# Dilated attention: values with v as the weights, two heads on the column halves of TensorE's array, output turned back by two transposes per double unit

## What is computed

```python
s = einsum('bnqche,bnkche->bnchqk', qs, kw) * scale + bias
s = where(mask, s, MASK_VALUE)
m = max(s, axis=-1)
e = exp(s - m)
l = sum(e, axis=-1)
o = einsum('bnchqk,bnkche->bnqche', e, vw)
o = o * (1 / l)
lse = m + log(l)
```

## Time and profile before

| | |
|---|---|
| median of 3 runs | 3131.64 us (3131.01 to 3131.96) |
| profiled execution | 3134.61 us, span 3132.8 us |
| mean granted TensorE clock | 0.977 |
| TensorE matmuls / weight loads | 2984.1 us (95%) / 2489.8 us (79%) |
| VectorE / ScalarE / POOL | 1656.2 (53%) / 1195.8 (38%) / 729.7 us (23%) |
| dilated attention on TensorE | 1392.9 to about 1751 us |
| its value matmuls (L1354) | 1280 records, 163.9 us |

### The profile page before, as it was taken

How to read it: one execution, slowest core, us unless ns; L and a number is a source line. 1 busy time by engine, 2 the same in 40 slices (tenths; PEclk the granted TensorE clock), 3 DMA queues, 4 the chain that set the end, 5 groups by cost and what they waited for, 6 DMA issues and landing times. The chain is left out here.

```text
span 3132.8 us, 47888 instructions
## 1 busy us (share of the span) xinstructions
PE 2984.1 (95%) x18330; PEld 2489.8 (79%) x18330; DVE 1656.2 (53%) x2757; ACT 1195.8 (38%) x2667; POOL 729.7 (23%) x576
## 2 busy tenths in 40 slices
PE   6999999999799999989999799899799999799998
PEld 6988888988588888878888678688688888667776
DVE  3366665000888888866666677433341100166665
ACT  3222221011577777755555321322211111255553
POOL 1234433110502010027452344200001110121111
PEclk9999999999899999999999899999899999899999
DMA  4212212223212010022332556332245542544341
GB/s 155 84 58 71 72 60 78 72 64 74 82 28 50 22 48 22 22 77 86 100 101 68 200 211 240 128 123 82 82 124 118 126 96 52 159 150 140 127 152 64
DMA packets 254270, 302.94 MB, mean 97 GB/s; under 512 B 19376, under 2 KB 201696, under 8 KB 250848
## 3 DMA queue, kind: packets, MB, share of 16 engines
q1 hardware_dynamic: 254048, 299.92, 31.7%
HBM read 190.38 MB, written 109.47 MB: 96 GB/s over the span
## 5 line engine op out<-in xcount | busy, mean ns | idle before, releaser
L890 DVE CUSTOM_DVE_ANT_0 d_e<-d_score,d_dist,d_slope 128x1024 f32<-128x1024 f32 x256 | 318.5, 1281 | 62.9 <-PE d_score L953 62.9
L561 PE MATMUL p_acc<-p_h_hi,p_w_hi 128*128 128x512 f32 x768 | 300.0, 391 | 1.0 <-issue 1.0
L561 PE MATMUL p_acc<-p_h_hi,p_w_lo 128*128 128x512 f32 x768 | 299.5, 390 | 0.0
L561 PE MATMUL p_acc<-p_h_lo,p_w_hi 128*128 128x512 f32 x768 | 299.1, 389 | 0.0
L812 ACT ACTIVATE d_e<-d_e,d_neg_top 128x2048 f32<-128x2048 f32 x128 | 257.0, 2008 | 86.5 <-DVE d_neg_top L899 86.2
L504 DVE RECIPROCAL p_root<-p_root 128x512 f32<-128x512 f32 x64 | 214.6, 3353 | 123.0 <-ACT p_root L417 123.0
L976 PE MATMUL d_out<-d_v,d_w_t 128*128 128x128 f32 x2048 | 251.5, 277 | 0.0
L976 PEld LDWEIGHTS d_out<-d_v,d_w_t 128*128 128x128 f32 x2048 | 240.9, 194 | 0.0
L561 PE MATMUL s_acc<-s_h_hi,s_w_hi 128*128 128x512 f32 x576 | 224.7, 390 | 0.0
L561 PE MATMUL s_acc<-s_h_hi,s_w_lo 128*128 128x512 f32 x576 | 224.4, 390 | 0.0
L561 PE MATMUL s_acc<-s_h_lo,s_w_hi 128*128 128x512 f32 x576 | 224.4, 390 | 0.0
(11 more groups left out here) (277 smaller groups left out, 6907.4 us busy)
## 6 DMA issues: line engine op xcount, KB each, us to landing
k_carry<-in_w_in SPq DMA_DIRECT2D x16, 1024.0 KB, 6.0
cols<-k_carry SPq DMA_DIRECT2D x64, 256.0 KB, 2.4
w_q<-q SPq DMA_DIRECT2D x15, 1024.0 KB, 7.8
k_carry<-x SPq DMA_DIRECT2D x27, 512.0 KB, 3.6
o_parts<-l_stage SPq DMA_DIRECT2D x192, 66.0 KB, 1.7
m_o<-o_parts SPq DMA_DIRECT2D x48, 264.0 KB, 6.0
k_carry<-cols SPq DMA_DIRECT2D x48, 256.0 KB, 4.6
k_carry<-in_a_w_in SPq DMA_DIRECT2D x10, 1024.0 KB, 5.6
```

Of the source, the lines that this page charges most:

```text
L561: mm = pe.matmul(acc[:, room], w_part[:, j, kt, ct * P:(ct + 1) * P], h_part[:, kt, tc * BANK:(tc + 1) * BANK], start=(kt == 0 and m == 0) ...
L890: dve.tensor_tensor_reduce(e[:, m % 3, s, half * HALF:(half + 1) * HALF], score[:, 2 * half:2 * half + 2].rearrange("p a b -> p (a b)"), d ...
```

## The change

The operands of the value matmuls change places: `v[level][:, chunk + k, own]` (128 keys x 64 channels) is the weight, `e_t` (128 keys x 128 queries) streams. Head h writes the partitions of its half, `own`, so that the two heads stand on the two column halves of the array. `out` now holds channels x queries for both units (`WIN` = 256 columns). VectorE copies it to the new tile `by_channel`; two transposes turn it back into the second half of the same bank; a second copy goes to `stage`. These steps run one round later, and the loops of VectorE and TensorE are a round longer. Two semaphores are new.

```diff
+        by_channel = ph.sb("by_channel", [P, WIN])
...
             def move_out(n):
                 dve.wait_ge(valued, 2 * n + 2)
+                if n >= 1:
+                    dve.wait_ge(turned_back, n)
+                dve.tensor_copy(by_channel[:, :], out[:, n % 2, 0:WIN]).then_inc(out_moved, 1)
+
+            def stage_out(n):
+                dve.wait_ge(turned_back, n + 1)
                 dve.tensor_copy(stage[:, 2 * n % SLOTS:2 * n % SLOTS + 2, 0:2 * HD],
-                                out[:, n % 2, 0:4 * HD].rearrange("p (u n) -> p u n", u=2)).then_inc(staged, 1)
-
-            for n in range(-1, TOTAL + 1):
+                                out[:, n % 2, WIN:2 * WIN].rearrange("p (u n) -> p u n", u=2)).then_inc(staged, 1)
+
+            for n in range(-1, TOTAL + 2):
+                if n >= 2:
+                    move_out(n - 2)
                 if n + 1 < TOTAL:
                     top(n + 1)
+                if n >= 2:
+                    stage_out(n - 2)
                 if 0 <= n < TOTAL:
                     for u in (2 * n, 2 * n + 1):
                         if not moved_by_act(u):
                             move(u)
-                if n >= 1:
-                    move_out(n - 1)
...
-                for h in range(2):
-                    for k in range(w):
-                        mm = pe.matmul(out[:, n % 2, (2 * j + h) * HD:(2 * j + h + 1) * HD], e_t[:, u % 4, w * h + k],
-                                       v[level][:, chunk + k, h * HD:(h + 1) * HD], start=(k == 0), stop=(k == w - 1))
+                for k in range(w):
+                    for h in range(2):
+                        own = slice(h * HD, (h + 1) * HD)
+                        mm = pe.matmul(out[own, n % 2, j * P:(j + 1) * P], v[level][:, chunk + k, own],
+                                       e_t[:, u % 4, w * h + k], start=(k == 0), stop=(k == w - 1))
                 mm.then_inc(valued, 1)

-            for n in range(-1, TOTAL + 1):
+            def turn_back(n):
+                pe.wait_ge(out_moved, n + 1)
+                for j in range(2):
+                    mm = pe.transpose(out[:, n % 2, WIN + j * P:WIN + (j + 1) * P], by_channel[:, j * P:(j + 1) * P],
+                                      ident[:, :])
+                mm.then_inc(turned_back, 1)
+
+            for n in range(-1, TOTAL + 2):
                 if n + 1 < TOTAL:
                     scores(n + 1)
+                if n >= 2:
+                    turn_back(n - 2)
                 for j in range(2):
                     if 0 <= n < TOTAL:
                         transposes(2 * n + j)
-                    if n >= 1:
+                    if 1 <= n <= TOTAL:
                         values(2 * n - 2 + j)
```

More of the change, by code:

```diff
@@ L1097, in dilated_attention @@
         valued = ph.sem("valued")
+        out_moved = ph.sem("out_moved")
+        turned_back = ph.sem("turned_back")
         staged = ph.sem("staged")
```

## The result

The changed kernel takes 3147.6 us (median of 7 runs, 3139.2 to 3156.3) against 3132.0 (3129.0 to 3139.1). The ratio is 1.0045, 95% interval 1.0029 to 1.0061: 9 to 19 us slower, 14 in the middle. The forecast was 19 us slower, at the edge of that interval, and 3150.5 us in all, 2.9 above the median and with it in the range of 3143 to 3170. The profiled executions differ by more than the ratio says, 3148.9 against 3132.8 us of span; 15.5 of these 16.1 us lie in dilated attention (first to last record: 1385.0 to 1751.5 before, 1386.0 to 1767.9 after), 1.0 came before it and the rest of the kernel gave back 0.3. What is outside is scatter: over the kernels of this study, in which the stages ahead of dilated attention are all the same, it starts anywhere between 1378.5 and 1389.2 us. So the stage's own length and its steps say more than a total.

The account below looks back on a forecast made before the run. TensorE's own queue was taken to bound the stage. Two-tile steps +2.6, single-tile steps +15.0 and the end +1.0 gave +18.6, say +19 us, on 3131.6: 3150.5 us, range 3143 to 3170.

Parts of the forecast that it names:

- What bounds the stage: Dilated attention: TensorE's own queue alone sets its time, matmuls filling 348.2 of 348.8 us.
- The change of division: TensorE's array: after a change the next group starts 0.07 us before the last matmul's recorded end, instead of 0.28.
- The pace of a pair: Value matmuls on the column halves: 0.115 us a pair, so groups take 0.60 us (4 pairs) or 0.37 (2).
- Two-tile steps: The 64 steps with two key tiles: 2.60 instead of 2.56 us from scores to bias, +0.04 each, +2.6 us.
- Single-tile steps: The 32 steps with one key tile: 1.70 instead of 1.23 us from scores to bias, +0.47 each, +15.0 us.
- The end: After the last values group: two transposes and a second copy are added before the store, +1.0 us.
- What was costed at nothing: VectorE's 96 more copies, 0.42 us each, 40 us in the stage, stay covered with 0.7 us slack; DMAs unchanged.
- Rival 1: Changes of division into or out of column halves cost nothing, values overlap as now: -42 us, 3090 us; chance 0.06.
- Rival 2: Value pairs do not keep 0.115 us at 128 columns: +29 us (3179) or +67 us (3217); chance 0.07.
- rival 3: VectorE's chain through by_channel becomes late in the fullest steps: some 3157 to 3163 us; chance 0.04.
- theory A: Follow-up runs: how often TensorE changes its array's division decides; a way into the column halves and out costs some 0.29 us.
- rival C: Run with e_t split into query halves: a pair never goes below about 0.11 us, ratio about 1.01; no chance given.

Follow-up runs that it names:

- the two-step blocks: Two kernels, mixed old/new value forms and e_t split into query halves, with two steps' values in one block instead of one step's: 1.0040 and 0.9944 to before.
- grouped_new: Changed kernel with both units' transposes together, then both units' values, entering the column halves once a step: 3121.7 us, 0.9961 to the kernel before.
- grouped_old: Kernel before the change, values in their old form, with the same regrouping (all transposes of a step, then all values): 1.0013 to the kernel before.
- heads_outer: Changed kernel with value matmuls in the other order, both key tiles of head 0, then both of head 1: 1.0049 to the kernel before.

## Why the prediction was right, point by point

- **What bounds the stage: right.** In the steps it is TensorE's queue and nothing else; every edit above moved the stage by what it did to that queue, until the two-step blocks uncovered ScalarE and the stores.
- **The change of division: right.** The same distance as in the window stage's rows, now between transposes and values: 1451.70 + 0.60 = 1452.30, next group 1452.22. Halving the number of changes gave back 0.30 us a step (4.14 - 3.84 and 3.26 - 2.96). The Trainium skill, page "TensorEngine Tiling (Array Packing)", section "Key Properties", says that changing the tiling mode drains the engine. The trace agrees: the loader stands idle for 0.17 us at each way in and each way out.
- **The pace of a pair: 5% too long.** Forecast 0.115, measured 0.109: grouped_new has 1453.98 to 1455.00 for 8 pairs, the changed kernel 1452.22 to 1452.81 for 4, in the median 1.025 and 0.588, and 0.437/4 = 0.109. The nearest row was the window stage's 0.107, not the row halves' 0.12. 640 pairs x 0.006 take 4 us off, and the way in and out, 0.15 and not 0.14, puts some 2 back. Together the groups of 4 pairs take 0.588 us for 0.60, those of 2 pairs the 0.37 forecast: 128 x 0.012 = 1.5 us, half of the miss of 3 us in the stage (18.6 against 15.5). The rest is some 0.01 us a step in the transposes and in the rounding of the starts.
- **Two-tile steps: forecast +0.04 each, measured 0.00** (-2.6 us). At 4.14 us they lie just below the 4.15 to 4.20 that were named as a sign of being right. **Single-tile steps: forecast +0.47, measured 3.263 - 2.807 = +0.46** (14.6 of 15.0 us).
- **The end: forecast +1.0.** The stage grew 15.5 us, 14.6 by single-tile steps, so 0.9 is left for its start and end together. The sum fits, but the path is not the whole one: the forecast had one way round behind the last values, and the trace has TensorE waiting for by_channel in two rounds before that as well, 0.53 us each. What took that back was not traced.
- **What was costed at nothing: right.** VectorE's 96 added copies cost nothing in the steps; TensorE waited for by_channel at the stage's end alone. The slack was larger than the forecast 0.7 us: the copy was done 0.94 to 1.03 us before TensorE asked in most steps and 0.60 at the least. VectorE's busy time grew by 21 us and not by 40, since neighbouring records overlap (at 1452.67 and 1453.01 us two start 0.34 apart, and the first is 0.41 long).
- **Rival 1** (changes that cost nothing, -42 us) falls with the 0.17 us holes and with grouped_new. **Rival 2** fell with the pace, **rival 3** with the waits.
- **A slip in the sum:** 3131.6 + 19 is 3150.6, not 3150.5. Nothing hangs on it.

## What to carry to other kernels

Before putting small matmuls on parts of TensorE's array, count the changes of division that this adds to the queue, and price each by a place of the same profile that already has one; put all the work of one division together before doubling its rate. Where the streaming side is 64 wide, splitting the weight itself into two column halves puts two records side by side as swapping the operands does, and the output needs no turning back (here 0.9914 against 0.9961, both with the values in one block). Once the groups are together, ask which engine feeds the rounds that have become short.

## What the runs showed that was not expected

- Values over two steps lost instead of gaining a little more: 1.0040 and 0.9944 where 0.992 and 0.987 were forecast by theory A.
- Expected by one theory of its run alone (about 0.06, against rival C's 0.11): a pair of 64-column weights with a 64-column stream takes 0.058 us in fp32, half of the 0.109 with a 128-column stream.
- The run had left it open: two independent groups on the two column halves run side by side in either queue order (heads_outer, +0.01 us a step).
- Transposes that follow full-array values start some 0.05 us earlier than a bias matmul at the same place (0.84 against 0.89 us in the earlier trace rows, +0.04 us a step in grouped_old). What makes the difference was not tried.
